# A hybrid encoder block in fp32: output gate, gated unit and taps for token block 0 alone ahead of its row gathers, and the dense work of block 1 and of blocks 2 and 3 in two passes beside them

## The reference, cut to what matters

```python
h = _rmsnorm(x, norm1_g[l])
proj = h @ w_in[l]
q, k, v, og, gkf, gkb, glu, ga, gb = jnp.split(proj, offsets, axis=-1)
...
o = (o_f + o_b).transpose(0, 2, 1, 3)            # two scans of gated linear attention, 4 heads
o = _rmsnorm(o, gla_onorm_g[l])
o = (o * jax.nn.silu(og.reshape(B, S, GLA_HEADS, GLA_DV))).reshape(B, S, GLA_VAL_WIDTH).astype(x.dtype)
y_a = o @ gla_w_o[l]
a_in, a_gate = jnp.split(glu, 2, axis=-1)
u = a_in * jax.nn.sigmoid(a_gate)
u = lax.conv_general_dilated(u, conv_w[l][:, None, :], ...) + conv_b[l]     # 31 taps along the tokens
u = jax.nn.silu(_layernorm(u, conv_ln_g[l], conv_ln_b[l]))
y_b = u @ conv_w_pw2[l]
merged = jax.nn.sigmoid(ga) * y_a + jax.nn.sigmoid(gb) * y_b
x = x + merged @ w_out[l]
h2 = _rmsnorm(x, norm2_g[l]).reshape(B * S, D)
x = x + _peer(h2, peer_w_q[l], peer_keys[l], peer_u[l], peer_v[l]).reshape(B, S, D)
```

## Time and profile before

| what | value |
|---|---|
| median of 3 runs | 4854.55 us (4849.68 to 4869.43) |
| the profiled execution | 4858.68 us, of which the span of its instructions is 4856.9 us |
| PE busy | 4126.5 us, 85% of the span |
| DVE busy | 2403.1 us, 49% |
| ACT busy | 785.5 us, 16% |
| POOL busy | 1318.2 us, 27% |
| moved by DMA | 1379.18 MB, 284 GB/s over the span |
| queue of the row gathers | 1073.81 MB |
| queue of the weight slabs | 293.87 MB |
| mean granted clock of PE | 0.956 |

### The profile page before, as it was taken

One profiled execution on the slowest core, in us unless ns is written; L12 is line 12 of the kernel. 1 busy time (PEld: TensorE's weight loads), 2 busy tenths in 40 slices (PEclk: granted clock), 3 DMA queues, 4 the chain that ended last, 5 costly groups with the idle time before them and its releaser, 6 DMA issues. The chain is left out here.

```text
span 4856.9 us, 34657 instructions
## 1 busy us (share of the span) xinstructions
PE 4126.5 (85%) x10596; PEld 1938.6 (40%) x10596; DVE 2403.1 (49%) x3280; ACT 785.5 (16%) x1990; POOL 1318.2 (27%) x1070
## 2 busy tenths in 40 slices
PE   7999999999999899999994388888767777777775
PEld 3444444444433565555542234433223233333332
DVE  1222111377741156656667866667444445444544
ACT  1221212100010211111102111211111111111112
POOL 0000000000010015433345433333334444444442
PEclk9999999999999999999997699999999999999998
DMA  2211111112267668999999899999999999999998
GB/s 103 84 50 55 69 52 69 52 69 86 78 256 272 251 259 346 360 353 379 366 364 355 319 368 378 381 360 362 376 384 414 418 422 416 416 418 422 417 418 343
DMA packets 183069, 1379.18 MB, mean 284 GB/s; under 512 B 23111, under 2 KB 23239, under 8 KB 24265
## 3 DMA queue, kind: packets, MB, share of 16 engines
q0 software_dynamic: 147456, 1073.81, 54.9%
q1 hardware_dynamic: 33056, 293.87, 15.7%
q10 hardware_dynamic: 2508, 10.91, 0.7%
HBM read 1374.32 MB, written 4.19 MB: 284 GB/s over the span
## 5 line engine op out<-in xcount | busy, mean ns | idle before, releaser
L1693 PE MATMUL bank<-arena_c 128*128 128x512 f32 x2048 | 970.2, 624 | 325.8 <-ACT arena_c L855 313.3
L1411 PE MATMUL bank<-arena_h,wring 128*128 128x512 f32 (+2 forms) x3200 | 1108.4, 508 | 28.6 <-DVE arena_c L1247 7.1
L1330 DVE SCALAR_TENSOR_TENSOR arena_h<-arena_h,arena_c 128x2048 f32<-128x2048 f32 x256 | 585.5, 2293 | 588.6 <-DMA arena_h<-in_peer_u,arena_c 581.2
L555 POOL DMA_INDIRECT arena_c<-in_peer_v,arena_c x512 | 620.6, 1212 | 660.5 <-DVE arena_h L1330 339.9
L1411 PEld LDWEIGHTS bank<-arena_h,wring 128*128 128x128 f32 x3200 | 569.9, 192 | 563.4 <-issue 395.5
L1693 PEld LDWEIGHTS bank<-arena_c 128*128 128x128 f32 x2048 | 389.7, 198 | 906.4 <-ACT arena_c L855 476.9
L1198 DVE SCALAR_TENSOR_TENSOR arena_c<-arena_c 128x2048 f32<-128x2048 f32 x256 | 586.2, 2290 | 250.3 <-DMA arena_c<-in_peer_u,arena_c 242.1
L551 POOL DMA_INDIRECT arena_c<-in_peer_u,arena_c x256 | 353.6, 1381 | 1310.6 <-DVE arena_c L1198 917.0
L1659 PE MATMUL bank<-arena_c,arena_h 128*128 128x512 f32 x1024 | 495.5, 633 | 136.7 <-ACT arena_h L823 115.3
L1440 PE MATMUL bank<-wring,arena_h 128*128 128x512 f32 x1024 | 443.7, 594 | 1.6 <-issue 1.0
L1659 PEld LDWEIGHTS bank<-arena_c,arena_h 128*128 128x128 f32 x1024 | 201.6, 202 | 407.3 <-issue 267.9
(11 more groups left out here) (190 smaller groups left out, 2640.3 us busy)
## 6 DMA issues: line engine op xcount, KB each, us to landing
wring<-in_w_in SPq DMA_DIRECT2D x72, 2048.0 KB, 7.7
wring<-in_gla_w_o SPq DMA_DIRECT2D x16, 2048.0 KB, 7.7
wring<-in_conv_w_pw SPq DMA_DIRECT2D x16, 2048.0 KB, 7.6
wring<-in_w_out SPq DMA_DIRECT2D x16, 2048.0 KB, 7.3
wring<-in_peer_w_q SPq DMA_DIRECT2D x16, 2048.0 KB, 8.6
arena_c<-in_peer_v,arena_c POOLq DMA_INDIRECT x512, 11.9
arena_c<-in_x SPq DMA_DIRECT2D x4, 1024.0 KB, 12.3
arena_o<-in_x ACTq DMA_DIRECT2D x4, 1024.0 KB, 11.4
```

What stands on the lines that cost most here:

```text
L555: pool.indirect_dma_start(out=v_rows[s], out_offset=None, in_=v_tab[0], in_offset=at)\
L1330: V.scalar_tensor_tensor(row, row, 1.0, block_of(h2, b), ALU.mult, ALU.mult, accum_out=act_u2[:, m, k:k + 1]).then_inc(u2_used, 1)
L1411: last = M(ps[bank][:, 0:hi - lo], w_slot(slot)[:, k, m * P:m * P + P], act_in[:, k, lo:hi], start=k == 0, stop=k == KT - 1)
L1693: last = M(ps[4 * m + q][:], diag[:, s, :], v2_row[s][:, q * 512:q * 512 + 512], start=k == 0, stop=k == TOP - 1)
```

## The change

The order of the stages is changed, for block 0 and for the rest.

- **Heads**: the output gate's projection leaves the head loop; the loop writes the normalized, ungated output to `oT`.
- **Block 0 alone**, before its gathers: value and gate of the gated unit for 143 tokens (128 and 15 that the taps reach into, `GL`), the taps for 128 tokens, the output gate for 128 tokens (`og0`), the LayerNorm on PE and ACT in place of POOL's sums, both branches from 32 slabs with the weights as the stationary operand (`tiles`, two tiles of 128 tokens in one PSUM bank), the output projection, the second norm, the queries, the top-16. The last 15 tokens of the unit that taps of block 1 need are kept in `u_keep`.
- **Beside units 0 to 15** (256 steps on DVE and ACT, written out one by one; a step's other work is in `beside(s)`): first, in 8 turns given by `TURN_AT`, value and gate for 384 tokens, their 31 taps spread over the turn's steps, the output gate (turns 0 to 3) and branch A of block 1 (turns 4 to 7); then the LayerNorm of three blocks, branch B of block 1 (steps 83 to 90), its output projection (to step 99), norm and queries (steps 105 to 120). From step 130 to 190 both branches of blocks 2 and 3 in 16 pairs of slabs, one pair every 4 steps; their output projection to step 208, norms, and the first queries at step 220.
- Units 0 to 15 add their v rows on DVE now, two steps behind the dot (`LAG`) where it was one. Units 16 to 23 go as units 8 to 15 went, with queries for two blocks in place of three. `SIDE` is 24 units, and the last 8 run with four u buffers.
- The last norm of blocks 0 to 2 and their stores go beside units 24 to 27.
- The keys come transposed from the host. Slabs of 2 MB loaded: 208, where it was 136; of these 88 ahead of the gathers (88 before, too) and 120 beside them (48 before).

```diff
-HEAD_SLABS = 6
...
+HEAD_SLABS = 4
...
-SIDE = 2 * PH
+SIDE = 3 * PH
+STEPS = 2 * PH * TOP
...
-PLAN_FIRST = ((0, 3, 8, 13), (0, 4, 9, 14))
-PLAN_3 = ((2, 7, 12), (4, 9, 14))
-PLAN_LAST = ((), (4,))
...
+LAG = 2
+TURN_AT = (0, 10, 20, 30, 40, 47, 54, 61, 68)
+OG_AT = (4, 7)
...
-                for first, bank0, done in ((2, 0, v_mm), (4, 4, og_mm)):
-                    if bank0:
-                        pe.wait_ge(z_dif, h * 4 + 4)
-                    for s in range(2):
-                        slab_ready(first + s, h, HEAD_SLABS)
-                        for k in range(KT // 2):
-                            kk = s * (KT // 2) + k
-                            for b in range(NB):
-                                last = M(by_half(ps[bank0 + b][:]), hT[:, kk, b * P:b * P + P], w_slot_half(s)[:, :, k, :],
-                                         start=kk == 0, stop=kk == KT - 1)
-                                if kk == KT - 1:
-                                    last.then_inc(done, 1)
-                        pe.drain().then_inc(w_used, 1)
+                for s in range(2):
+                    slab_ready(2 + s, h, HEAD_SLABS)
+                    for k in range(KT // 2):
+                        kk = s * (KT // 2) + k
+                        for b in range(NB):
+                            last = M(by_half(ps[b][:]), hT[:, kk, b * P:b * P + P], w_slot_half(s)[:, :, k, :],
+                                     start=kk == 0, stop=kk == KT - 1)
+                            if kk == KT - 1:
+                                last.then_inc(v_mm, 1)
+                    pe.drain().then_inc(w_used, 1)
...
+            def tiles(slot, act_in, bank, lo, hi, done):
...
+                w = hi - lo
+                for m in range(2):
+                    for k in range(KT):
+                        last = M(ps[bank][:, m * w:(m + 1) * w], w_slot(slot)[:, k, m * P:m * P + P],
+                                 act_in[:, k, lo:hi], start=k == 0, stop=k == KT - 1)
+                last.then_inc(done, 1)
...
+            pairs("glu0", SB_GLU0, hT, 0, GL)
...
+            def og0_slab(n):
+                slab_ready(SB_OG0 + n)
+                pe.wait_ge(og0["used"], n + 1)
+                tiles(n % 2, hT, n % 4, 0, P, og0["mm"])
+                slab_used()
+            for n in range(4):
+                og0_slab(n)
...
+            pairs("m0", SB_MA0, oT, 0, P)
+            pe.wait_ge(pair["m0"]["use"], 2 + 8)
+            pe.wait_ge(ln0["act"], KT)
+            pairs("m0", SB_MB0, cv, 0, P, 8)
...
+            def glu1(first, i, per, before, j):
+                p = pair["glu1"]
+                slab_ready(first, i, per)
+                for m in range(2):
+                    pe.wait_ge(p["use"], j * 2 + (2 * before + m + 1))
+                    project(0, m, hT, m, p["gate"], P, T)
+                slab_used()
+                slab_ready(first + 1, i, per)
+                for m in range(2):
+                    project(1, m, hT, 2 + m, p["val"], P, T)
+                slab_used()
...
+            def ma1(first, i, per, a, count):
+                p = pair["ma1"]
+                pe.wait_ge(p["use"], count)
+                slab_ready(first, i, per)
+                tiles(0, hT, 6 - 2 * a, P, 2 * P, p["gate"])
+                slab_used()
+                slab_ready(first + 1, i, per)
+                tiles(1, oT, 7 - 2 * a, P, 2 * P, p["val"])
+                slab_used()
...
+            glu1(SB_GLU1, 0, 2, 0, 0)
+            with pe.Fori(0, 4) as j:
+                for s in range(2):
+                    slab_ready(SB_OG1 + s, j, 4)
+                    for m in range(2):
+                        pe.wait_ge(og1["used"], j * 4 + (2 * s + m + 1))
+                        project(s, m, hT, 4 + 2 * s + m, og1["mm"], P, T)
+                    slab_used()
+                glu1(SB_OG1 + 2, j, 4, 1, j)
+            pe.wait_ge(og1["used"], 4 + KT)
+            with pe.Fori(0, 3) as j:
+                for a in range(2):
+                    ma1(SB_MA1 + 2 * a, j, 6, a, j * 2 + (a + 1))
+                glu1(SB_MA1 + 4, j, 6, 5, j)
+            for a in range(2):
+                ma1(SB_MA1_LAST + 2 * a, 0, 4, a, 6 + a + 1)
...
-                                           og_s[:, c, :], ALU.mult, ALU.mult).then_inc(o_norm, 1)
+                                           gbc_o[:, bass.ds(h * DV, DV)], ALU.mult, ALU.mult).then_inc(o_norm, 1)
...
+            def glu1_take(j):
...
+                for m in range(2):
+                    dve.wait_ge(p["val"], 2 * j + m + 1)
+                    dve.wait_ge(p["sig"], 2 * j + m + 1)
+                    V.tensor_tensor(upad1[:, m, PAD:PAD + T1], ps[2 + m][:, 0:T1], sig1[:, m, :], ALU.mult)\
+                        .then_inc(p["use"], 1)
...
+            def conv1(j, first, end):
+                for n in range(first, end):
+                    r, m = n // 2, n % 2
+                    dst = cv[:, 2 * j + m, P:T]
+                    tap = cols[:, 2 * j + m, R_CW + r:R_CW + r + 1]
...
+                        ins = V.scalar_tensor_tensor(dst, upad1[:, m, r:r + T1], tap, dst, ALU.mult, ALU.add)
...
+            def og1_scale(j, s):
+                for m in range(2):
+                    t = 4 * j + 2 * s + m
+                    dve.wait_ge(og1["sig"], t + 1)
+                    V.tensor_tensor(oT[:, t, P:T], ps[4 + 2 * s + m][:, 0:T1], oT[:, t, P:T], ALU.mult)\
+                        .then_inc(og1["used"], 1)
...
+            def beside(s):
+                for j in range(8):
+                    r, steps = s - TURN_AT[j], TURN_AT[j + 1] - TURN_AT[j]
+                    if r == 0:
+                        glu1_take(j)
+                    if j < 4 and r in OG_AT:
+                        og1_scale(j, OG_AT.index(r))
+                    if j >= 4 and r in IT_AT:
+                        ma1_merge(2 * (j - 4) + IT_AT.index(r))
+                    if 0 <= r < steps:
...
+            for U in range(2 * PH):
+                topk = None
+                if U >= PH - 1:
+                    head = U - (PH - 1)
+                    topk = parts_beside(topk_1(head) if head < PH else topk_2(0), 1)
+                for k in range(TOP):
+                    s = U * TOP + k
+                    if s >= LAG:
+                        add_row((s - LAG) // TOP, (s - LAG) // P, (s - LAG) % TOP)
+                    dot(U, s // P, k)
+                    beside(s)
+                    if topk:
+                        topk(k)
+                    if k == COPY_AT:
+                        V.tensor_copy(idx_cur[:, (U + 1) % 2, :], idx_all[:, U + 1, :]).then_inc(idx_ready, 1)
+            for k in range(TOP - LAG, TOP):
+                add_row(2 * PH - 1, 1, k)
...
+            two_units(NB - 1, 0, norm_beside([0, 1]))
+            two_units(NB - 1, 2, norm_beside([2]))
+            with dve.Fori(2, PH // 2) as j:
+                two_units(NB - 1, j * 2, lambda n: None)
```

1203 lines of the change are left out of this document (689 added, 514 removed).

## The result

The changed kernel takes 4775.9 us (median of 4 runs, 4765.6 to 4785.4), the kernel before 4856.6 us beside it (4849.7 to 4869.4): a ratio of 0.9824, 95% interval 0.9808 to 0.9839. Measured once more with other kernels of the study it took 4775.4 us and 0.9825 (0.9808 to 0.9843). The forecast was 4795 us.

A forecast was written before the change was run, and what follows sets the result against it. Row gathers and slabs sharing the DMA engines set the pace after a start-up time. Start -470, units 0 to 15 +312, units 16 to 23 +101, end -4: -61 us against the profiled span, forecast 4795 us, range 4700 to 4910.

The forecast's parts named there:

- Start, -470: Before the first gather: shorter heads and block 0 done alone let the gathers start at 1290 us instead of 1760.
- Steps 0 to 68, 639 us: Beside the first gathers: 344 us for steps 0 to 40 and 295 us for steps 40 to 68.
- The full rate, 385 GB/s: From step 68, wherever slabs are read, the DMA is the limit, at 385 GB/s.
- nearer to the busy case: Choice of 385 GB/s between 396 with DVE busy 10.2 of 12 us and 427 with 6.0.
- rival 2: The DMA-bound part runs at 420 GB/s instead of 385, 90 us less, 4705 us in all; chance 0.10.
- 536 us for steps 68 to 130: Beside the gathers: 44 steps with 39 slabs at the DMA's rate, 468 us, and 12 steps at 5.7, 68 us.
- Where no slab is read, two u buffers limit: In steps without slab loads the round of two u buffers sets the pace, 5.7 to 5.9 us a step.
- End, -4: After the last dot: three of four final norms move beside the gathers, the end coming 4 us better on balance.
- rival 1: In units 0 to 15 the shared DMA is no faster than before: about 361 GB/s, chance 0.20; 350 and below, 0.15.
- PE's clock: Sign that PE's clock stays above 0.9 in steps 83 to 120; half clock would add 30 to 60 us.
- The issues between taps: Sign that POOL's issues between the taps beside the gathers last below 2 us.
- rival 3: DVE is held by POOL's issues, two a step at 0.94 us each: 90 us more, 4885 us; chance 0.05.

The follow-up runs named there:

- three u buffers and the later sum: Changed kernel with three u and three v buffers (was two and four), and units 16 to 23's sums added behind the next unit's second dot: 4749.7 us.

## Why the prediction was right, and where not

- *Start, -470.* Right, by its own steps: -463. Of the 6 us, 1.8 are the first query, which took 9.22 us where the earlier trace rows had 7.41; its granted clock was 0.78 (0.97 before), and ahead of it PE had waited 7.1 us (5.0 before). Taps of 128 columns came at 344 ns on their own and at 0.293 us in sequence ((831.2 - 690.5) / 480), for 0.277.
- *Steps 0 to 68, 639 us.* 651. In steps 0 to 40 (343 us for 344) PE is the limit: halved slabs change nothing, and ten taps fewer only 9 us. Taps at 0.541 us for 0.535. The 12 us are in steps 40 to 68, where bytes count too (16 us less with halved slabs).
- *The full rate, 385 GB/s.* This is the term that was mis-sized. Measured 410 to 415 at a share of 0.99 to 1. The step that failed is "nearer to the busy case": I put the difference between the two windows of the earlier trace rows, 396 and 427 GB/s, down to VectorE, and the experiments find no loss of the full rate by VectorE (422 GB/s with it busy 27 of 30 us). 385 lies below both windows; what drew it down were whole stages at 360 and 366, of which PE limited the first and the second held a halt in each unit. What made the two windows of 12 us differ is not shown. Steps 68 to 209 took 1088 us, where 1151 were forecast. By the sign that the prediction had named (410 GB/s or more) this is rival 2; the rate was there, and the total was not 4705. The forecast of 536 us for steps 68 to 130 holds a slip, too: it counts 44 and 12 steps where there are 62. By its own prices 44 steps with 39 slabs are 452 us and the other 18 103, together 555; the slip hid 19 us of the wrong rate.
- *Where no slab is read, two u buffers limit.* The number held for units 16 to 23 (93.9 us each, forecast 90 to 95), the reason did not: with three u buffers and the later sum they take 91. It was read from a mean of 94 us that contains a halt at each unit's end, already in the kernel before: the last step of its units 8 to 15 takes 10.0 to 15.6 us, the others 5.4 on the mean. This is unit 8 of before (L1229 is the sum):

```profile
2869.55 2.29 DVE L1198 SCALAR_TENSOR_TENSOR arena_c<-arena_c 128x2048 f32<-128x2048 f32 x1 [3.90 <-DMA arena_c<-in_peer_u,arena_c]
...
2881.84 2.48 DVE L1229 TENSOR_TENSOR arena_o<-bank,arena_o 128x512 f32<-128x512 f32 x4 [9.99 <-PE bank L1659]
2885.01 2.29 DVE L1198 SCALAR_TENSOR_TENSOR arena_c<-arena_c 128x2048 f32<-128x2048 f32 x1 [0.69 <-DVEq L96]
```

  For steps 209 to 256 both failed, 302 us for 279. There VectorE is busy 193 of 227 us, and GpSimd 135 with 72 issues of 1.9 us, and dots beside the search come 7.4 to 8.3 us apart, for example these of after:

```profile
3268.41 2.28 DVE L1301 SCALAR_TENSOR_TENSOR arena_c<-arena_c 128x2048 f32<-128x2048 f32 x1
...
3273.58 2.35 DVE L1311 SCALAR_TENSOR_TENSOR arena_o<-arena_c,arena_o 128x2048 f32<-128x2048 f32 x1
3275.85 2.28 DVE L1301 SCALAR_TENSOR_TENSOR arena_c<-arena_c 128x2048 f32<-128x2048 f32 x1
```

  No idle time stands before them: dot, 2.9 us of search, added row make a step of 7.4 us that VectorE fills. Eleven of the 47 steps are filled so and take 7.6 us on the mean, 19 us more than eleven of 5.9; in six other long ones VectorE waits 2.8 to 5.4 us for rows, and what delays these is open. The 5.9 us came from units 8 to 15 of before, where PE adds the rows; here VectorE does both, and the prediction did not count that, though the second line of the earlier trace rows, from unit 7 of before, shows that case: VectorE busy 76.6 of 82 us. This is read from the traces; no run here took the search away.
- *End, -4.* The sign of its two halves is right: from the end of the last dot it takes 17.1 us for 31.4, 14 saved for the 13 of the forecast; beside the units 1.5 were lost for 10.
- *In sum.* From the first copy of indices to step 256 it took 2049 us for 2089, a mean of 379 GB/s for 371, with the break-even of rival 1 at 361. The span came to 4763.9 against 4795.5. Steps 68 to 209 gave 63 us, the first dot 6 and the tail 10; steps 40 to 68 took 13 back, 209 to 256 23, and the units behind them 13. So the total came within 32 us by errors of 80 and 49 us against each other, which is luck; the start and the steps to 40 came as worked out.
- *Signs.* PE's clock was to be above 0.9 in steps 83 to 120: it was 0.91 at first, then 0.71 and 0.84. With slabs halved steps 68 to 130 got 48 us shorter at much the same clock (0.87 for 0.83), so bytes and not the clock held them, for the most part. The issues between taps are below 2 us as forecast; rival 3 (VectorE pays for them) is out: the 140 dots (L1301) that started while an issue was running took 2.28 to 2.31 us.

**Where 463 us went.** The start gives 463, the tail 14. In the kernel before, the last 16 units went at 80.5 us with nothing beside them. Now only 8 do, at 81; units 16 to 23 take 13 us more each (107 in all), and units 0 to 15 take 270 us more than before: 100 us of gain are left less 7 in the last units, the 93 between the two spans. The dense work of blocks 1 to 3 was moved to where its bytes compete with the rows: halving all slab loads from there on gives 142 us back. The other half can't be worth as much, since with halved slabs PE is already busy 390 of 404 us in steps 130 to 190.

## What to carry over

Work moved beside a transfer-bound loop was paid mostly in bytes here: count its bytes at the full rate of the DMA engines, and look for stretches where neither the engines nor the DMA are full, because those may hold a halt. A mean per unit hides it; list the starts of one instruction through a unit before a buffer count is named as the limit. A difference between two windows is no price of the one column that comes to mind: here it gave VectorE 8%, and runs that load VectorE alone gave nothing where the DMA engines were full; what they cost was a longer halt at the end of each unit, and a window across units had hidden that as well.

## What was not expected of the hardware

- Gathers and slabs together moved 410 GB/s over 449 us, with VectorE busy 0.72 and PE 0.89 of the time; gathers alone moved 422 over 30 us with VectorE busy 0.90.
- An instruction that issues a gather lasted 1.0 to 3.6 us on the mean of a stage, and neither 3585 ns (steps 0 to 40 with fewer taps, PE-bound, 350 GB/s for 347) nor a GpSimd busy 26.3 of 30 us (422 GB/s) lengthened a step.
- An issue (0.94 us on its own) outlasted the instruction of VectorE under which it started, where this read two tiles or was a copy at 0.63 ns a column (to 0.8 us after a dot, through a second one if it follows at once: 5.29 us), and not for a reduction (69 of 69 at 0.94 to 0.95 us).
